# Half-row hand-overs between layers, a router's path folded into the last output unit, and one expert load issued earlier

## The chip, the cores and the metric

One NeuronCore of a Trainium2 chip runs the whole program, all in fp32. The metric is the device time of one execution in microseconds (us). The core's engines run from instruction queues of their own and wait for each other through semaphores: TensorE (PE, matrix products; PEld its weight loads), VectorE (DVE), ScalarE (ACT), GpSimd (POOL) and SyncE (SP), which here only issues DMA transfers. Products are written to PSUM, everything else lies in SBUF (128 partitions).

## The reference

A sequence of 256 tokens with 1024 channels passes through two blocks of two layers each. Cut to what matters:

```python
# first block, layer 0 (attention + SSM) and layer 1 (pooling); normed residual
for layer in range(2):
    y = mixer[layer](rmsnorm(x, pre_norm[layer]))        # products with w_in, w_out
    x = x + rmsnorm(y, post_norm[layer])
# second block
for layer in range(2):
    h = h + hybrid_mixer(rms_norm(h, norm1_g[layer]), ...)   # retention + HGRN2, w_in, w_out
    h = h + expert_choice_ffn(rms_norm(h, norm2_g[layer]), w_router, w_gate, w_up, w_down)
return rms_norm(h, final_norm_g)

def expert_choice_ffn(xn, w_router, w_gate, w_up, w_down):
    cap = 2 * s // 16                                    # 32 tokens for each of 16 experts
    affinity = softmax(xn @ w_router)
    gate, idx = top_k(swapaxes(affinity, 1, 2), cap)     # each expert chooses its tokens
    xe = gather(xn, idx)
    hid = silu(xe @ w_gate) * (xe @ w_up)
    ye = (hid @ w_down) * gate
    return scatter_add(ye, idx)
```

The weights of the 16 experts of one layer are 16 times 12 MB; each is used for 32 tokens only.

## The kernel before

The tokens lie as NT = 2 tiles of 128 rows (`x[:, i, :]`, i = 0, 1). Weights pass through a ring of 6 slots of 2 MB (`ring`), in "units": a unit is 2 MB (or 1 MB) of one weight matrix. Units 0 to 10 are even_w_in and the SSM's matrix, 11 to 13 even_w_out, 14 to 21 odd_w_in, 22 to 25 pool_w, 26 to 29 odd_w_out; FIRST2[l] (30 for layer 0 of the second block) starts nine units of w_in_2, OUT2[l] two of w_out_2, MOE[l] the 96 units of the experts (six for each: four of gate and up, two of down).

**Split units.** For nearly all dense units, weights and activations are split into a high part (rounded to fp32r) and a low part (the rest), and each product is three: L1475, L1476 and L1477. ScalarE makes the high part of a unit (`high_part`, L779, a 128x4096 copy), VectorE the low part (`low_part`, L1147). A split unit takes two ring slots. The first unit of layer 1 of the second block alone (`WHOLE`) is multiplied whole, in fp32 (L1492). A unit of output weights goes through `rows_unit`, in four quarters: token tile 0, columns 0 to 511 and 512 to 1023, then tile 1 the same.

**The seam between layers** of the first block (`norm_between`, on ScalarE L687, on VectorE L1001) comes after units 13 and 29. ScalarE squares and sums a row of the output in PSUM (`rms`, L681), VectorE scales it (L1005), adds it to x (L1008), ScalarE squares the sum, VectorE normalises into xs (L981), TensorE transposes xs (L1544) and VectorE makes the gained rows and their two parts (L993 product, L994 rounding, L995 subtraction) in `gain_out`. All of it whole rows of 1024, tile 0 and then tile 1.

**The router's path**, in each layer of the second block, comes after the second output unit. VectorE adds the output to x (L1369), TensorE transposes x (L1544, `transpose_rows`), VectorE applies the gain (L997), TensorE makes the logits (L1900), one tile after the other. Softmax (L1375 to L1379), transposes of the affinities (L1905), then the selection on VectorE (eight at a time, MAX8 and MATCH_REPLACE8, L1383 to L1388), transposes of the slot numbers (L1916), a copy (L1390), a comparison (`choose`, L1418) and the first gather on TensorE (L1927). TensorE also clears four PSUM banks by products with zeros (L1911), which stands between L1905 and L1916 in its queue.

**The experts.** Their units use the ring's 6 slots and three more (EXTRA) in the `work` area, which holds activations of the mixer until then. `load_moe` on SyncE issues the loads in the order of use; the three extra slots wait for `gm_sb` (both merges of the mixer's heads done), the first ring slots for the end of the units that used them, and every load from the tenth on for the end of the unit nine before. An expert is L1955 (gate and up, 32 instructions for each unit in the trace), L1927 for the next gather, L1980 (down) and L1992 (scatter).

**What sets the order.** Each engine's order is written out by hand. TensorE's smaller steps are hung into the dense units at fixed quarters (`ahead_of`, `slots`).

## Time and profile before

| | us |
|---|---|
| median of 3 runs | 1712.32 |
| lowest and highest of them | 1712.03, 1713.57 |
| profiled execution, own time | 1711.37 |
| its span | 1709.6 |
| TensorE busy | 1333.4 (78%) |
| VectorE busy | 559.1 (33%) |
| ScalarE busy | 424.6 (25%) |
| bytes moved by DMA | 516.38 MB, mean 302 GB/s |

The span lies 1.8 us below the execution's own time. Times in the rows are microseconds from the span's start. A row of the timeline gives start, duration, engine, line, operation and shapes; in brackets stands how long the engine was idle before it and what ended that. Chains are read by laying the end of one engine's row beside the start of the next engine's. TensorE's instructions are pipelined, so that rows overlap by some tenths.

The page's chain that ended last goes to 47% through DMA transfers (nearly all of them expert weights) and to 39% through TensorE.

### The profile page before, as it was taken

Reading aid. Unit: us, or ns where it says so; the run is one execution under the profiler, and the core shown is the slowest. Engines: PE = TensorE matmul, PEld = TensorE weight load, DVE = VectorE, ACT = ScalarE, POOL = GpSimd, SP = SyncE. Lnnn points to the kernel's source line nnn. Section 1 sums busy time; section 2 is a strip of 40 time slices with the busy share of each in tenths; the row PEclk is TensorE's granted clock in tenths of the full one; section 3 lists DMA queues with packets and bytes.
Section 4 is the critical chain, followed back from the end, with each engine's and each line's share of the span. In section 5 each row is a group of like instructions: output and inputs, shape, how many; then the busy total and the mean of one; then the engine's idle time right before and its main releaser. Section 6 shows DMA issues by size and latency. Waiting matters only on the chain.

```text
span 1709.6 us, 28214 instructions
## 1 busy us (share of the span) xinstructions
PE 1333.4 (78%) x12496; PEld 923.3 (54%) x12496; DVE 559.1 (33%) x790; ACT 424.6 (25%) x538; POOL 136.4 (8%) x155
## 2 busy tenths in 40 slices
PE   7999889999899987665665666999986666566564
PEld 5688767998798853232322233788843223223232
DVE  8855775455566430000000001485520000000001
ACT  5236334443465311000101011455210101000011
POOL 0120300000304000000000000204000000000000
PEclk9999999999999989798889887999989888888886
DMA  9134243564443699999999999333799999999996
GB/s 326 51 124 148 111 164 114 174 219 149 147 149 124 245 398 426 424 428 425 427 425 427 426 426 411 133 137 133 286 408 425 426 427 424 428 424 428 425 426 264
DMA packets 86148, 516.38 MB, mean 302 GB/s; under 512 B 6336, under 2 KB 6464, under 8 KB 53056
## 3 DMA queue, kind: packets, MB, share of 16 engines
q1 hardware_dynamic: 82576, 509.20, 73.3%
q0 software_dynamic: 992, 3.42, 0.6%
q10 hardware_dynamic: 2512, 2.75, 0.5%
q8 instruction: 55, 0.90, 0.2%
q14 instruction: 13, 0.11, 0.0%
HBM read 514.30 MB, written 1.05 MB: 301 GB/s over the span
## 4 chain that ended last, share of the span: by engine, by line
DMA 47%; PE 39%; DVE 6%; POOL 2%; ACT 2%; issue 2%; SPq 1%; DVEq 0%; ACTq 0%; POOLq 0%
DMA ring<-in_w_down 24%; DMA ring<-in_w_gate 20%; PE dense L1475 8%; PE dense L1477 8%; PE dense L1476 8%; PE bank L1955 3%; DMA ring<-in_w_up 2%; PE dense L1492 2%; PE bank L1980 2%; DMA ring<-in_even_w_in 1%; PE bank L1814 1%; DVE ring_parts L1147 1%; POOL work L655 1%; PE bank L1900 1%; PE dense L1911 1%
## 5 line engine op out<-in xcount | busy, mean ns | idle before, releaser
L1955 PE MATMUL bank<-ring,work 128*32 128x256 f32 x2688 | 203.3, 457 | 143.9 <-DMA ring<-in_w_up 87.7
L1955 PEld LDWEIGHTS bank<-ring,work 128*32 128x32 f32 x2688 | 92.3, 126 | 249.6 <-DMA ring<-in_w_up 108.5
L1147 DVE TENSOR_TENSOR ring_parts<-ring,ring_parts 128x4096 fp32r<-128x4096 f32 (+1 forms) x44 | 184.1, 4194 | 115.8 <-ACT ring_parts L779 115.7
L951 ACT ACTIVATE work<-bank 128x256 f32<-128x256 f32 x32 | 12.3, 384 | 750.5 <-PE bank L1955 750.5
L1407 DVE TENSOR_TENSOR work<-work,bank 128x256 f32<-128x256 f32 x32 | 13.5, 421 | 563.0 <-ACT work L951 563.0
L779 ACT ACTIVATE ring_parts<-ring 128x4096 fp32r<-128x4096 f32 (+1 forms) x45 | 154.1, 3432 | 96.2 <-DMA ring<-in_w_in 40.4
L1955 PE MATMUL bank<-work 128*32 128x256 f32 x1408 | 105.8, 454 | 71.2 <-DMA work<-in_w_up 45.1
L1980 PE MATMUL bank<-ring,work 128*32 128x256 f32 x1344 | 91.8, 419 | 59.6 <-DMA ring<-in_w_down 54.9
L1475 PE MATMUL dense<-xT_parts,ring_parts 128*128 128x256 f32 x448 | 129.5, 289 | 2.7 <-DVE ring_parts L1147 2.7
L1477 PE MATMUL dense<-xT_parts,ring_parts 128*128 128x256 f32 x448 | 126.8, 283 | 0.0
L1955 PEld LDWEIGHTS bank<-work 128*32 128x32 f32 x1408 | 49.9, 127 | 124.8 <-DMA work<-in_w_up 55.7
L1476 PE MATMUL dense<-work_parts,ring_parts 128*128 128x256 f32 x400 | 113.2, 283 | 0.0
L1477 PE MATMUL dense<-ring_parts,work_parts 128*128 128x512 f32 x288 | 112.9, 392 | 0.0
L664 POOL TENSOR_TENSOR work<-work 128x128 f32<-128x128 f32 x64 | 24.2, 399 | 933.9 <-PE bank L1963 782.2
L1980 PEld LDWEIGHTS bank<-ring,work 128*32 128x32 f32 x1344 | 43.0, 119 | 100.5 <-DMA ring<-in_w_down 67.2
L1412 DVE COPY work<-bank 128x256 f32<-128x256 f32 x32 | 13.6, 424 | 228.6 <-PE bank L1980 228.6
L1475 PEld LDWEIGHTS dense<-xT_parts,ring_parts 128*128 128x128 f32 x448 | 85.9, 192 | 3.6 <-ACT work L699 3.1
L1477 PEld LDWEIGHTS dense<-xT_parts,ring_parts 128*128 128x128 f32 x448 | 85.9, 192 | 0.0
L1475 PE MATMUL dense<-ring_parts,xT_parts 128*128 128x512 f32 x176 | 72.9, 414 | 8.9 <-DVE xs_parts L995 3.9
L1476 PEld LDWEIGHTS dense<-work_parts,ring_parts 128*128 128x128 f32 x400 | 76.7, 192 | 0.4 <-issue 0.2
L1475 PE MATMUL dense<-ring_parts,work_parts 128*128 128x512 f32 x176 | 69.9, 397 | 2.3 <-ACT work L704 2.3
L1476 PE MATMUL dense<-ring_parts,xT_parts 128*128 128x512 f32 x176 | 69.7, 396 | 0.0
(325 smaller groups left out, 2202.5 us busy)
## 6 DMA issues: line engine op xcount, KB each, us to landing
ring<-in_w_gate SPq DMA_DIRECT2D x42, 2048.0 KB, 41.0
ring<-in_w_up SPq DMA_DIRECT2D x42, 2048.0 KB, 41.0
ring<-in_w_down SPq DMA_DIRECT2D x42, 2048.0 KB, 40.8
work<-in_w_gate SPq DMA_DIRECT2D x22, 2048.0 KB, 40.6
work<-in_w_up SPq DMA_DIRECT2D x22, 2048.0 KB, 40.7
work<-in_w_down SPq DMA_DIRECT2D x22, 2048.0 KB, 41.1
ring<-in_w_in SPq DMA_DIRECT2D x18, 2048.0 KB, 8.6
ring<-in_even_w_in SPq DMA_DIRECT2D x10, 2048.0 KB, 10.6
```

The lines of the kernel that those rows point to most:

```text
L655: g.tensor_tensor(x1, t4[0], t4[1], ALU.subtract).then_inc(rot_done, 1)
L664: g.tensor_tensor(wsel[:, i], csel[:, i:i + 1, :].to_broadcast([P, 4, CAP]), aff[:, i, bass.ds(e, 1)].unsqueeze(2).to_broadcast([P, 4, CAP ...
L779: s.activation(slot_of(u, True)[0], slot_of(u), ACT.Copy).then_inc(hi_done, 1)
L1147: tt(lo, slot_of(u), hi.bitcast(F32), ALU.subtract).then_inc(lo_done, 1)
L1475: mm(o, x_parts[0], y_parts[0], start=start, stop=False)
L1476: mm(o, x_parts[0], y_parts[1], start=False, stop=False)
L1477: return mm(o, x_parts[1], y_parts[0], start=False, stop=stop)
L1492: last = mm(d[:, i, :], act_T[:, k, i, :], w[:, k, :], start=k == 0, stop=k == nk - 1)
L1814: last = mm(o, x_, y_, start=True, stop=True)
L1900: last = mm(WB[0][:, NE * i:NE * i + NE], xT[:, k, i * P:(i + 1) * P], wr[:, l, k, :], start=k == 0, stop=k == DC - 1)
L1955: last = mm(WB[0][32 * q:32 * q + 32, 256 * (j % 2):256 * (j % 2) + 256], xeT[:, 4 * (j // 2) + k, :], w[:, k * D + 256 * q:k * D + 256 * ...
L1980: last = mm(WB[3][32 * r:32 * r + 32, 0:256], hidT[:, b, 32 * q:32 * q + 32], w[:, at:at + 256], start=q == 0 and b == 0, stop=q == 3 and ...
```

## The change

Five pieces.

1. **Half rows in `norm_between`.** Squares, scaling and addition run by halves of 512 columns, `half_ps` and `sum_half` announce the first ones; a half's sum enters the second half's root as its bias. In `gain_out` VectorE only makes the product and the subtraction; the rounding copy goes to ScalarE (`gain_high`). `normalise` writes two halves, and `transpose_rows` waits for each.
2. **The seam between the two layers of the second block**: the first unit (`WHOLE`) starts when tile 0's rows are gained (`full_ready`); tile 1's transposes stand inside it, the roundings and subtractions behind all four products.
3. **The router's path**: `rows_unit` of the last output unit takes eight transposes of tile 0 ahead of its fourth quarter, and ahead of that quarter's last k (`late`) tile 0's logits and half of tile 1's transposes. The clearing of the PSUM banks takes fp32r operands and stands before the affinities' transposes. The first choice is compared straight from PSUM. Tile 1's scaling stands between softmax and selection.
4. **Expert loads**: the load j = 4 (FIRST_IN) is issued ahead of the output units and waits for `ho_ps`; the loads into the other two extra slots wait for the end of the mixer's last input unit and for the first merge. `rgT` and `hgT` are moved out of those slots.
5. **The output** leaves in two transfers, one for each tile.

```diff
-        rgT = area(13312, "p (h s) -> p h s", h=RH, s=S)
-        hgT = area(14336, "p (h s) -> p h s", h=RH, s=S)
+        rgT = area(4096, "p (h s) -> p h s", h=RH, s=S)
+        hgT = area(11264, "p (h s) -> p h s", h=RH, s=S)
...
-                        sp.wait_ge(gm_sb, 4 * (l + 1))
+                        sp.wait_ge(*((unit_done, OUT2[l]), (gm_sb, 4 * l + 2), (ho_ps, l + 1))[s - RING])
...
+                FIRST_IN = RING - 2
+                load_moe(0, FIRST_IN)
+                for u in range(OUT2[l], MOE[l]):
+                    load(u)
                 for j in range(6 * TURN_E):
-                    load_moe(j // 6, j)
+                    if j != FIRST_IN:
+                        load_moe(j // 6, j)
...
+                dense_rms(0)
+                sum_rms(0)
+                dense_rms(1)
+                gain_high(0, at)
+                sum_rms(1)
+                gain_high(1, at)
+
+            def rms_halves(i, of, first, second):
+
+                act.wait_ge(*first)
+                own.link(s.activation(xs[:, i, 0:512], of[:, 0, :], ACT.Square, accum_out=stat[:, 7, 0:1]))
+                own.go(s.activation(stat[:, 7, 1:2], stat[:, 7, 0:1], ACT.Identity, scale=1.0 / D, bias=eps[:]))
+                act.wait_ge(*second)
+                own.link(s.activation(xs[:, i, 512:1024], of[:, 1, :], ACT.Square, accum_out=ssq[:, i:i + 1]))
+                s.activation(std[:, i:i + 1], ssq[:, i:i + 1], ACT.Sqrt, scale=1.0 / D, bias=stat[:, 7, 1:2]).then_inc(std_ready, 1)
...
-                for i in range(NT):
-                    if i == 0:
-                        dve.wait_ge(tile0_ps, 3 + l)
-                    else:
-                        dve.wait_ge(unit_done, MOE[l])
-                    tt(x[:, i, :], x[:, i, :], DP[i][:].rearrange("p b n -> p (b n)"), ALU.add).then_inc(x_ready, 1)
-                    gain_out(i, f"n2_{l}")
-                for i in range(NT):
-                    normalise(i)
-                v.memset(zeros, 0.0).then_inc(zero_set, 1)
+                tt(zeros, ident, ident, ALU.subtract).then_inc(zero_set, 1)
+                dve.wait_ge(tile0_ps, 3 + l)
+                add_half(0, 0)
+                add_half(0, 1)
+                dve.wait_ge(half_ps, 6 + 2 * l)
+                add_half(1, 0)
+                gain_out(0, f"n2_{l}")
+                normalise(0)
+                dve.wait_ge(unit_done, MOE[l])
+                add_half(1, 1)
+                gain_out(1, f"n2_{l}")
+                inverse(1)
...
+                ts(xs[:, 1, :], x[:, 1, :], rstd[:, 1:2], None, ALU.mult).then_inc(xs_ready, 2)
...
-                              [[], [], [at(mix_transposes, 0)], []] if n == 0 else ())
+                              [[], [], [at(mix_transposes, 0)], []] if n == 0 else [[], [], [], [first_rows]],
+                              [[], [], [], [first_logits]] if n else ())
+                rows_half(1, 1)
+                logits(1, 0)
+                logits(1, 1).then_inc(lg_ps, 1)
```

**TensorE, router's path.** Before, from the end of the last output unit to the transposes of the slot numbers (bank, dense: PSUM; x: the tokens; wr: router weights; con, work: constants and activations):

```order
L1544 MATMUL bank<-con,x 128x128 x8
L1900 MATMUL bank<-wr,xT 128x16 x8
L1544 MATMUL bank<-con,x 128x128 x8
L1900 MATMUL bank<-wr,xT 128x16 x8
L1905 MATMUL bank<-con,work 16x128 x2
L1911 MATMUL dense<-xT,work 128x512 x4
L1916 MATMUL bank<-con,work 128x16 x2
```

Of the change, the same stretch, from the first logits, which now stand inside that unit:

```order
L1959 MATMUL bank<-wr,xT 128x16 x8
L1948 MATMUL bank<-con,x 128x128 x4
L1541 MATMUL dense<-ring_parts,work_parts 128x512
L1542 MATMUL dense<-ring_parts,work_parts 128x512
L1543 MATMUL dense<-ring_parts,work_parts 128x512
L1948 MATMUL bank<-con,x 128x128 x4
L1959 MATMUL bank<-wr,xT 128x16 x8
L2003 MATMUL dense<-work_parts 128x512 x4
L2008 MATMUL bank<-con,work 16x128 x2
L2013 MATMUL bank<-con,work 128x16 x2
```

Tile 0's logits and four of tile 1's transposes stand ahead of the unit's last three products (eight more transposes stand a quarter earlier), and the clearing (L1911, now L2003) has changed places with the affinities' transposes.

**VectorE, first seam, tile 0.** Before, from the first reciprocal to the last low part:

```order
L976 RECIPROCAL rstd<-std 128x1
L1005 SCALAR_TENSOR_TENSOR xs<-dense,rstd,row 128x1024
L1008 TENSOR_TENSOR x<-x,xs 128x1024
L976 RECIPROCAL rstd<-std 128x1
L981 TENSOR_SCALAR xs<-x,rstd 128x1024
L993 TENSOR_TENSOR xs<-bank,vec 128x512
L994 CAST xT_parts<-xs 128x4x128
L995 TENSOR_TENSOR xs_parts<-xs,xT_parts 128x512
L993 TENSOR_TENSOR xs<-bank,vec 128x512
L994 CAST xT_parts<-xs 128x4x128
L995 TENSOR_TENSOR xs_parts<-xs,xT_parts 128x512
```

Of the change:

```order
L1008 RECIPROCAL rstd<-std 128x1
L1044 SCALAR_TENSOR_TENSOR xs<-dense,rstd,row 128x512
L1050 TENSOR_TENSOR x<-x,xs 128x512
L1044 SCALAR_TENSOR_TENSOR xs<-dense,rstd,row 128x512
L1050 TENSOR_TENSOR x<-x,xs 128x512
L1008 RECIPROCAL rstd<-std 128x1
L1015 TENSOR_SCALAR xs<-x,rstd 128x512 x2
L1025 TENSOR_TENSOR xs<-bank,vec 128x512 x2
L1034 TENSOR_TENSOR xs_parts<-xs,xT_parts 128x512 x2
```

The two rounding copies (CAST) have left VectorE's queue, and the scaling and the addition stand in two halves each.

**SyncE, loads around the output units of layer 0.** Before:

```order
L549 DMA ring<-in_w_out_2 128x4x1024 x2
L580 DMA ring<-in_w_gate_2 128x4096
L580 DMA ring<-in_w_up_2 128x4096
L580 DMA work<-in_w_gate_2 128x4096
L580 DMA work<-in_w_up_2 128x4096
L580 DMA work<-in_w_down_2 128x2x2048
```

Of the change:

```order
L587 DMA work<-in_w_down_2 128x2x2048
L555 DMA ring<-in_w_out_2 128x4x1024 x2
L587 DMA ring<-in_w_gate_2 128x4096
L587 DMA ring<-in_w_up_2 128x4096
L587 DMA work<-in_w_gate_2 128x4096
L587 DMA work<-in_w_up_2 128x4096
```

One load of down weights has moved ahead of the two loads of output weights.

## Rows read from the trace of the kernel before

**Rows 1.** Page, part 2: busy share of the 16 DMA engines in 40 slices, in tenths.

```profile
DMA  9134243564443699999999999333799999999996
```

**Rows 2.** Timeline, VectorE, first seam (before unit 14): start, us, line, out<-in, [idle before].

```profile
245.86 1.28 DVE L1005 SCALAR_TENSOR_TENSOR xs<-dense,rstd,row 128x1024 f32<-128x1024 f32 x1
247.18 1.23 DVE L1008 TENSOR_TENSOR x<-x,xs 128x1024 f32<-128x1024 f32 x1
...
250.21 0.75 DVE L981 TENSOR_SCALAR xs<-x,rstd 128x1024 f32<-128x1024 f32 x1
251.71 0.69 DVE L993 TENSOR_TENSOR xs<-bank,vec 128x512 f32<-128x512 f32 x1 [0.75 <-PE bank L1544]
...
252.90 0.69 DVE L995 TENSOR_TENSOR xs_parts<-xs,xT_parts 128x512 fp32r<-128x512 f32 x1
...
254.69 0.69 DVE L995 TENSOR_TENSOR xs_parts<-xs,xT_parts 128x512 fp32r<-128x512 f32 x1
...
264.32 0.69 DVE L995 TENSOR_TENSOR xs_parts<-xs,xT_parts 128x512 fp32r<-128x512 f32 x1
```

**Rows 3.** Timeline, ScalarE: full-row square in that seam, half-row square elsewhere.

```profile
248.44 1.06 ACT L681 ACTIVATE xs<-x 128x1024 f32<-128x1024 f32 x1 [2.88 <-DVE x L1008]
...
539.75 0.60 ACT L919 ACTIVATE rtmp<-bank 128x512 f32<-128x512 f32 x1
```

**Rows 4.** Second seam: ScalarE's timeline; then waits of TensorE, 445 to 590 us.

```profile
442.50 3.61 ACT L779 ACTIVATE ring_parts<-ring 128x4096 fp32r<-128x4096 f32 x1
...
PE dense L1475 <- DVE ring_parts L1147: 2.7, 1, 2.7
```

**Rows 5.** Windows of that first seam: busy (count) by engine, then PEclk, DMA share, GB/s.

```profile
255.00:258.00 3.00, 2.56 (x6) 2.08 (x7) 2.93 (x4) 0.00 (x0) 0.00 (x0) 0.50 0.55 214
```

**Rows 6.** Timeline, TensorE, first layer's path from the last output unit to the experts.

```profile
599.62 1.03 PE L1544 MATMUL bank<-con,x 128*128 128x128 f32 x8
...
601.60 2.27 PE L1900 MATMUL bank<-wr,xT 128*128 128x16 f32 x16 [0.94 <-DVE xT L997]
...
606.44 3.60 PE L1900 MATMUL bank<-wr,xT 128*128 128x16 f32 x16 [0.78 <-DVE xT L997]
...
612.23 5.84 PE L1911 MATMUL dense<-xT,work 128*128 128x512 f32 x8
...
618.93 2.02 PE L1927 MATMUL bank<-xs,work 128*32 128x256 f32 x16 [0.64 <-DVE work L1418]
...
622.54 3.66 PE L1955 MATMUL bank<-ring,work 128*32 128x256 f32 x64 [0.60 <-DVE work L1401]
```

**Rows 7.** Timeline, VectorE, the same path.

```profile
612.48 0.42 DVE L1383 MAX8 work<-bank 16x8 f32<-16x256 f32 x1 [0.69 <-PE bank L1905]
...
617.35 0.41 DVE L1388 TENSOR_TENSOR work<-work 16x256 f32<-16x256 f32 x1
```

**Rows 8.** Timeline, SyncE's queue: first load that waits for an expert's slot.

```profile
624.53 0.33 SPq L580 DMA_DIRECT2D ring<-in_w_up  x1
```

**Rows 9.** Windows on that path: busy (count) by engine, then PEclk, DMA share, GB/s.

```profile
616.00:618.00 2.00, 2.00 (x4) 0.50 (x2) 1.66 (x4) 0.00 (x0) 0.00 (x0) 0.82 1.04 442
622.00:624.00 2.00, 1.46 (x28) 0.98 (x32) 0.53 (x2) 0.00 (x0) 0.00 (x0) 1.00 0.52 221
```

**Rows 10.** Timeline, TensorE, expert stage: two units of 32 products.

```profile
746.45 3.59 PE L1955 MATMUL bank<-ring,work 128*32 128x256 f32 x32 [2.96 <-DMA ring<-in_w_gate]
751.34 1.93 PE L1955 MATMUL bank<-ring,work 128*32 128x256 f32 x32 [1.30 <-DMA ring<-in_w_up]
```

**Rows 11.** Between the layers: TensorE's timeline, then VectorE's.

```profile
1071.19 14.00 PE L1492 MATMUL dense<-ring,xs 128*128 128x512 f32 x32 [1.20 <-DVE work_parts L995]
...
1074.63 4.42 DVE L1147 TENSOR_TENSOR ring_parts<-ring,ring_parts 128x4096 fp32r<-128x4096 f32 x1
```

**Rows 12.** DMA issues by line: out<-in, count, KB each, median us to landing.

```profile
x<-in_x SPq DMA_DIRECT2D x2, 512.0 KB, 4.1
...
out<-xs SPq DMA_DIRECT2D x1, 1024.0 KB, 4.1
```

168 lines of the change are left out of this document (113 added, 55 removed).

## The prediction

> **What bounds the kernel now.** Read first the page's row of DMA shares [rows 1]: digits of 9 from slice 15 to 24 and from 30 to the end are the two expert stages, in which the 16 DMA engines never rest. All before and between them is bound by TensorE and by the hand-overs between engines, the "seams". Second, the timeline of each seam: what stands between the last product of one unit and the first of the next. Third, SyncE's queue: when the expert loads are released.
>
> In an expert stage nine slots of 2 MB are filled ahead, and each further load waits until TensorE has finished with a slot. The first that waits is issued at 624.53 [rows 8]; in the window around it the DMA share drops to 0.52 [rows 9]. So nine slots were full and the stream stood still: the stage's end follows the moment of TensorE's first finished expert unit, not the moment of the first load.
>
> **The seams before units 14 and 30 (norm, add, norm).** The chain per token tile is: ScalarE squares, VectorE scales and adds, ScalarE squares the sum, VectorE normalises, TensorE transposes, VectorE makes gained rows in two parts.
> - Squares: 1.06 for a row, 0.60 for a half [rows 3]. The first half now runs while the second is still being made: -0.46, twice.
> - VectorE: 1.28 + 1.23 + 0.04 between them [rows 2] = 2.55. Four halves at 0.69, 0.65, 0.69, 0.65 (0.69 is the half-row price of L993 in the same rows; 0.65 is half of 1.23 and 0.04 of start) and three gaps of 0.04 make 2.80: +0.25.
> - Normalising: 0.75 for a row [rows 2]; the transposes of the first half may begin after some 0.41: -0.34.
> - Gained rows: from 251.71 to 254.69 + 0.69 = 3.67 [rows 2], for six instructions. Now two products and two subtractions, four times 0.72 = 2.88, with the rounding copies on ScalarE at 0.60 beside them: -0.8.
>
> Tile 0: -0.46 + 0.25 - 0.46 - 0.34 - 0.8 = -1.8. For tile 1 the first square was already done ahead: -1.35. Tile 0's copies stand in ScalarE's queue behind tile 1's first statistics, which costs some 0.15. Sum -3.0. Does it reach TensorE? In the first seam TensorE takes tile 1's rows when the last VectorE instruction ends (264.32 + 0.69 [rows 2]). In the second, TensorE later waited 2.7 for the low part of unit 31 (L1147) whose high part starts at 442.50, right behind the last VectorE instruction of the seam [rows 4]. So both pass on the whole: **-6.0** for two seams. Bounds: -4.0, if the halves cost 0.25 more per instruction pair than I take, and -7.5: the clock stood at 0.50 in 255 to 258 after the long pause [rows 5], which is TensorE's 1.2 of 2.4 GHz, and a shorter pause may leave it at 1.00 (it then gains little, since VectorE's tile 1 ends last).
>
> **The router's path, once per layer.** Before: the last output product ends near 599.85, its start pipelined into the transposes of 599.62, the logits end at 606.44 + 3.60 = 610.04, the selection runs from 612.48 to 617.35 + 0.41 = 617.76, the first gather starts at 618.93 and the first expert unit ends near 624.5 [rows 6 to 8].
> - TensorE now puts eight transposes (1.03), tile 0's logits (2.27) and four more transposes (0.5) [rows 6] inside the last output unit, which so ends at 599.85 + 3.8 = 603.65. What follows is short: half a row added (0.65), four transposes (0.5 at full clock, 0.95 at half), half a row gained (0.69), the last eight logits rows (half of 2.27 or of 3.60 [rows 6]). Logits end at 607.1 at full clock, 608.7 at half: -2.95 or -1.35.
> - One scaling (0.75 [rows 2]) now stands before the selection, beside two transposes that took about as long: +0.1.
> - Selection to gather took 618.93 - 617.76 = 1.17. The zeroing ended at 618.07 (612.23 + 5.84 [rows 6]), later than the selection, and no longer stands there (0.3); the first choice is now read straight from PSUM, without the copy ahead (0.1): -0.4.
>
> So the gather starts 1.65 (half clock) or 3.25 (full clock) sooner. I weigh them 2 to 1, since the second logits took 3.60 where the first took 2.27, the work between them being as thin as it will be: -2.2. **But the zeroing was also what brought the clock back.** It began at 0.50 and ended at 1.00: the window 616 to 618 has 0.82 [rows 9]. Now it is short and stands before the selection; TensorE then has nothing for over 5 us. Nearest row for a start after idleness: 32 products take 3.59 after 2.96 us of waiting, 1.93 at full clock [rows 10]. A gather of 2.02 [rows 6] at that ratio is 3.76: +1.75; two transposes at the same ratio some +0.25; the first expert unit +0 to +1.7, taken as +0.15, since the gather's own work comes first. Penalty +2.15. Net **-0.1 for both layers**; bounds +2.05 and -3.25 each.
>
> The Trainium skill ("TensorE: Matmul & The Clock Gate", Part 1, what is actually happening) says that the slow clock is the default and that activity releases it, idleness brings it back. The rule speaks against moving the zeroing; rows 9 and 10 agree with it. By the opposite assumption, a clock that stays, the path would give -3.25 a layer.
>
> **The extra slot.** One expert load goes ahead of the output weights, two more no longer wait for the second merge. That fills the ring some 6 us earlier, but the ring was already full when the first unit ended [rows 8, 9], so it earns nothing by itself: 0. It only raises the cap on what a faster router could earn (0.96 us of idle DMA in the window 622 to 624, and about as much until the load of 624.53 gets going). Its 2 MB stand ahead of the first output weights (4.8 us at the 442 GB/s of rows 9), which ScalarE splits at 550 and VectorE not before 565: hidden.
>
> **Between the layers.** TensorE's first unit (14.00 [rows 11]) now starts after tile 0's two products on VectorE alone. The two roundings and two subtractions between them fall away (3.6 to 1.45, as in the first seam) and the transposes begin 0.34 sooner: start -2.5. Tile 1's eight transposes move inside it (+1.0), and it starts with less work ahead of it, so partly at half clock: for a time between nothing and the 4.5 us of the zeroing, taken as 2.4, which costs +1.2. VectorE's low part for the next unit (4.42 [rows 11]) comes after four roundings that now stand later, and ends about when the unit does. Net **-0.3**; bounds -1.7 and +1.3.
>
> **The end.** Output in two halves: 1 MB landed in 4.1, but so did 0.5 MB at the start [rows 12]. Half of the bytes at 442 GB/s are 1.2 less; bounds 0 and -1.4. I take **-1.0**.
>
> **Sum.** The profiled execution took 1711.37 (span 1709.6). -6.0 - 0.1 - 0.3 - 1.0 = -7.4: 1704.0. The median of the runs shown, 1712.32, lies 0.95 above it, so I predict **1704.9** (ratio 0.9957). About 0.2% (3.4 us) is what a measurement of this kernel can tell from no change.
>
> **Rivals.**
> 1. *The router's path wins in full* (the clock holds, or comes back within the gather). For it: TensorE is busier through the logits than before. Against: over 5 us of idleness before the gather. -3.25 instead of -0.05, twice: 1704.9 - 6.4 = 1698.5. Chance 0.15.
> 2. *Half clock up to the first expert unit* in both layers: +2.05 instead of -0.05, twice: 1704.9 + 4.2 = 1709.1. For it: row 746.45 stays slow to its end [rows 10]. Against: the clock came back after some 4.5 us of work, between 612.23 and 616.7 (0.82 in the window from 616 [rows 9]). Chance 0.22.
> 3. *The halves earn half*: instruction overhead eats the seams, 1704.9 + 3 = 1707.9. Against: half-row prices are in the rows. Chance 0.08.
> 4. *Slower than before*: the unit between the layers starts on a cold array and stays at half clock. At its price of 14.00 for the whole unit at full clock, each us at half clock costs 0.5; the whole unit would add 14.0 - 1.2 = 12.8: 1717.7. It decides from some 17 us at half clock (7.4 saved elsewhere is used up at 14.8 beyond my 2.4); the return at 612 took 4.5. Chance 0.03.
> 5. *The forecast*, 1702 to 1708: chance 0.52.
>
> The range takes in 1 and most of 2: **1698.5 to 1709.5**. Faster by over 0.2% (below 1708.9): 0.52 + 0.15 + 0.08 + about half of case 2, less a little: 0.82. Within 0.2%: 0.14. Slower: 0.04.
>
> **What would show it.** Seams: the last subtraction of the first seam ends 3 us sooner after the start of its first scaling, and the start of unit 31 has moved with the second one. Router: logits end 10 to 11.6 us after the third quarter of the last output unit's products instead of 13; the gather takes 3 to 4 us, not 2.0; SyncE's first waiting load comes about as long after the output unit's third quarter as before (some 27.4 us). If the gather still takes 2.0, rival 1 is right. Extra slot: a longer gap of the DMA before the first expert unit ends, not a shorter stage. I am wrong if a waiting engine that I left out ends last: ScalarE between tile 1's statistics and tile 0's copies, or VectorE's low part behind unit 31 or between the layers.

## The result, and the profile after

| | before | after |
|---|---|---|
| median, us | 1713.57 (5 runs, 1712.03 to 1716.78) | 1703.57 (5 runs, 1700.19 to 1706.39) |
| profiled execution; its span | 1711.37; 1709.6 | 1706.39; 1704.5 |
| VectorE, ScalarE busy | 559.1, 424.6 | 558.3, 433.9 |

The ratio is 0.9945, 95% interval 0.9922 to 0.9967: the changed kernel is 9.4 us faster, with an interval from 5.7 to 13.4. I had forecast 1704.9 and a ratio of 0.9957. The total is right, but its terms are not. Two seams that I had put at -3.0 each gave -1.2 and -2.6. The router's path, which I had put at -0.1 for both layers, is the largest term: -4.8 in these two profiles.

The DMA row of the page of the changed kernel, which answers [rows 1], has an 8 in slices 15 and 30, the first of each expert stage, where a 9 stood before (before, the first stage's nines are slices 15 to 25, not to 24 as I wrote):

```profile
DMA  9134334455354589999999999444689999999996
```

**First seam**, timeline of the changed kernel, VectorE on tile 1 (it answers [rows 2]). Columns: start and duration in us, engine, line, operation, out<-in, count, and in brackets the idle time before and what ended it.

```profile
264.46 1.29 DVE L1025 TENSOR_TENSOR xs<-bank,vec 128x512 f32<-128x512 f32 x2 [0.37 <-PE bank L1615]
265.85 1.29 DVE L1034 TENSOR_TENSOR xs_parts<-xs,xT_parts 128x512 fp32r<-128x512 f32 x2
269.97 8.76 DVE L1190 TENSOR_TENSOR ring_parts<-ring,ring_parts 128x4096 fp32r<-128x4096 f32 x2 [2.82 <-ACT ring_parts L811]
```

ScalarE at the same place:

```profile
265.19 1.23 ACT L725 ACTIVATE xT_parts<-xs 128x512 fp32r<-128x512 f32 x2 [2.31 <-DVE xs L1025]
266.32 7.13 ACT L811 ACTIVATE ring_parts<-ring 128x4096 fp32r<-128x4096 f32 x2
```

TensorE, the first product of unit 15:

```profile
274.54 0.47 PE L1541 MATMUL dense<-ring_parts,xT_parts 128*128 128x512 f32 x1 [1.50 <-DVE ring_parts L1190]
```

Two products and two subtractions take 1.29 + 1.29 here, and VectorE's chain is as much shorter as I had worked out: from the start of ScalarE's square of tile 0's last half (before: of its row) to the end of tile 1's last subtraction it took 20.90 before and takes 17.84 now. But VectorE then stands still for 2.82, because the high part of unit 15 (the first of the two of 266.32) is made only behind the copies of 265.19, and TensorE waits 1.50 at the start of unit 15. In the kernel before this wait does not exist.

**Second seam.** Before, ScalarE stood still ahead of two sigmoids (L858, L859) that wait for a subtraction on VectorE (L1254) behind the whole seam, and only then made the high part of [rows 4]:

```profile
442.29 0.21 ACT L858 ACTIVATE lbt<-lbt 128x4 f32<-128x4 f32 x1 [4.27 <-DVE lbt L1254]
```

ScalarE's timeline in the changed kernel (it answers the first line of [rows 4]):

```profile
441.08 1.24 ACT L725 ACTIVATE xT_parts<-xs 128x512 fp32r<-128x512 f32 x2 [2.29 <-DVE xs L1025]
442.33 1.28 ACT L890 ACT_TABLE_LOAD   x1
443.62 0.21 ACT L890 ACTIVATE lbt<-lbt 128x4 f32<-128x4 f32 x1
443.74 0.19 ACT L891 ACTIVATE lbt<-lbt 128x4 f32<-128x4 f32 x1
443.83 7.12 ACT L811 ACTIVATE ring_parts<-ring 128x4096 fp32r<-128x4096 f32 x2
```

VectorE's low parts for units 31 and 32 behind it:

```profile
447.48 8.76 DVE L1190 TENSOR_TENSOR ring_parts<-ring,ring_parts 128x4096 fp32r<-128x4096 f32 x2 [4.36 <-ACT ring_parts L811]
```

The one wait of TensorE between 440 and 470 (total us, times, longest), as in [rows 4]:

```profile
PE dense L1541 <- DVE ring_parts L1190: 3.1, 1, 3.1
```

And a window behind it: busy time of PE, PEld, DVE, ACT and POOL with counts, granted clock, DMA share, GB/s.

```profile
452.00:455.00 3.00, 2.95 (x14) 2.98 (x15) 3.00 (x1) 0.00 (x0) 3.00 (x1) 0.50 1.05 406
```

The wait ahead of unit 31 has grown from 2.7 to 3.1: a table load of 1.28 and two sigmoids stand between the copies and the high part of unit 31. Before, the same table load ran while ScalarE waited in any case. Behind the wait the clock was at 0.50.

**Router's path**, first layer, TensorE's timeline (it answers [rows 6]):

```profile
606.90 2.09 PE L1959 MATMUL bank<-wr,xT 128*128 128x16 f32 x16
608.83 2.05 PE L2003 MATMUL dense<-work_parts 128*128 128x512 f32 x4
616.83 0.39 PE L2013 MATMUL bank<-con,work 16*128 16x16 f32 x2 [5.38 <-DVE work L1439]
617.63 2.05 PE L2024 MATMUL bank<-xs,work 128*32 128x256 f32 x16 [0.41 <-DVE work L1442]
620.29 0.69 PE L2033 MATMUL bank<-con,work 128*128 128x128 f32 x2 [0.61 <-DVE work L1450]
621.57 5.64 PE L2052 MATMUL bank<-ring,work 128*32 128x256 f32 x64 [0.60 <-DVE work L1455]
```

SyncE's first load that waits for an expert's slot ([rows 8]):

```profile
625.27 0.33 SPq L587 DMA_DIRECT2D ring<-in_w_up  x1
```

Three windows up to it ([rows 9]):

```profile
619.30:621.30 2.00, 1.07 (x6) 0.29 (x2) 0.71 (x2) 0.00 (x0) 0.00 (x0) 0.50 0.08 33
621.30:623.30 2.00, 1.73 (x19) 0.82 (x23) 0.27 (x2) 0.00 (x0) 0.00 (x0) 0.50 0.00 0
623.30:625.30 2.00, 2.00 (x24) 0.97 (x20) 0.00 (x0) 0.00 (x0) 0.00 (x0) 0.50 0.00 0
```

The second logits took 2.09 instead of 3.60. The gather of 617.63 ran at a granted clock of 0.50 and took 2.05, not the 3.76 of my forecast. The first expert unit did run slow, 5.64 instead of 3.66. The DMA rests for 6 us ahead of the load of 625.27 (its share was 0.48 in 618 to 620 and 0.00 from 622).

**Between the layers**, TensorE's unit with tile 1's transposes inside ([rows 11]):

```profile
1067.59 6.27 PE L1558 MATMUL dense<-ring,xs 128*128 128x512 f32 x8 [0.78 <-DVE xs L1505]
1073.69 1.04 PE L1615 MATMUL bank<-con,xs 128*128 128x128 f32 x8
1074.57 10.46 PE L1558 MATMUL dense<-ring,xs 128*128 128x512 f32 x24
```

A window in its first quarter:

```profile
1067.00:1070.00 3.00, 2.41 (x3) 1.18 (x4) 1.49 (x4) 1.85 (x1) 0.00 (x0) 0.50 1.04 384
```

**The end**, timeline of SyncE's two output transfers and of VectorE's last instruction:

```profile
1700.07 1.75 SPq L603 DMA_DIRECT2D out<-xs  x2
1700.15 1.28 DVE L1519 SCALAR_TENSOR_TENSOR xs<-x,rstd,row 128x1024 f32<-128x1024 f32 x1
```

The unit between the layers took 6.27 + 10.46 = 16.7 of products where it took 14.00 before; its first quarter ran at half clock.

### The stretches

Every engine's order is fixed, so a stretch between two marks can be compared over all traces. The marks: S1 and S2, the start of ScalarE's square that tile 0's last half (before: its row) releases at the first and second seam; Q0 and Q1, the start of ScalarE's square of tile 0 in each router's path (L681, after: L694). All in us, each the difference of two starts in one trace (the end of a unit is the start of the copy that it releases; the last row ends with the span, which is known to a tenth); "again" is a second profile of the kernel before (run e5).

| stretch | before | again | after | e1 | e2 | e3 | e4 |
|---|---|---|---|---|---|---|---|
| start to S1 | 244.12 | 245.22 | 249.30 | 248.68 | 247.38 | 246.42 | 248.22 |
| S1 to the first copy of a pool product (in unit 15) | 30.77 | 30.78 | 29.57 | 30.23 | 29.56 | 29.57 | 29.42 |
| S2 to unit 31's first product | 29.43 | 29.43 | 26.83 | 28.90 | 26.84 | 26.83 | 23.60 |
| S2 to the head norms' root (stat 128x8), 155 us on | 156.76 | 156.78 | 155.46 | 157.70 | 155.65 | 154.13 | 150.84 |
| Q0 to the first waiting load | 28.84 | 28.85 | 26.87 | 24.78 | 24.91 | 24.74 | 24.74 |
| Q1 to the same in layer 1 | 27.79 | 27.62 | 24.94 | 25.02 | 24.94 | 24.90 | 24.99 |
| that load to TensorE's last landed weights, layer 0 | 431.93 | 432.37 | 432.10 | 432.33 | 433.04 | 432.08 | 432.05 |
| the same, layer 1 | 433.37 | 434.34 | 433.36 | 433.28 | 434.33 | 433.36 | 433.36 |
| ScalarE's statistics to the end of the unit between the layers | 21.50 | 23.30 | 22.55 | 22.95 | 23.05 | 23.02 | 22.64 |
| last statistics (first square) to the end | 9.01 | 8.94 | 7.55 | 7.56 | 7.57 | 7.59 | 7.55 |

Between these rows lie stretches that the change does not touch. From the first seam's mark in unit 15 to S2, from the head norms to Q0 and from the unit between the layers to Q1 they repeat within 0.25; from the last landed weights to ScalarE's statistics they read 5.2 to 7.3 in the first layer and 5.2 to 7.8 in the second. The code there is the same in all kernels, and what differs is the granted clock under the last expert units: before, it was at 0.50 from 1057.0 on, after, at 1.00 until 1062.5.

Because of the clock the two profiles must not be compared as a whole. From S1 on they differ by 10.3. Of this 2.8 lie in those last stretches (7.3 and 5.2, 7.8 and 7.1). In the other direction the changed kernel had half clock for 4.0 us of its first expert unit (2.1 longer), as no other trace has, and in unit 31 (1.3 longer than in e3). The latter befell three of the six traces that wait ahead of unit 31 (after, e1, e2) and none of the six that do not (e4 and all on top of it).

### The profile page after: what moved, and what is told of

It is laid out like the page before. It is cut to its first block, busy times and chain, and to the rows that moved or that the text cites. A ratio compares the mean times of both kernels' runs of the same rounds, so it can differ in the third digit from the quotient of the medians.

```text
span 1704.5 us, 28251 instructions
## 1 busy us (share of the span) xinstructions
PE 1323.7 (78%) x12488; PEld 920.2 (54%) x12488; DVE 558.3 (33%) x804; ACT 433.9 (25%) x570; POOL 139.1 (8%) x155
## 4 chain that ended last, share of the span: by engine, by line
DMA 47%; PE 40%; DVE 5%; POOL 2%; ACT 2%; issue 2%; SPq 1%; DVEq 0%; ACTq 0%; POOLq 0%
DMA ring<-in_w_down 25%; DMA ring<-in_w_gate 22%; PE dense L1541 8%; PE dense L1543 8%; PE dense L1542 8%; PE dense L1558 2%; PE bank L2052 2%; PE bank L2077 2%; DVE ring_parts L1190 1%; PE dense L1575 1%; ACT ring_parts L811 1%; DMA ring<-in_even_w_in 1%; PE bank L1888 1%; POOL work L668 1%; PE bank L1760 1%
## 5 line engine op out<-in xcount | busy, mean ns | idle before, releaser
L2052 PE MATMUL bank<-ring,work 128*32 128x256 f32 x2688 | 204.6, 459 | 157.3 <-DMA ring<-in_w_up 95.8
L2052 PE MATMUL bank<-work 128*32 128x256 f32 x1408 | 105.6, 454 | 66.4 <-DMA work<-in_w_up 42.2
L2077 PE MATMUL bank<-ring,work 128*32 128x256 f32 x1344 | 84.0, 391 | 52.7 <-DMA ring<-in_w_down 43.9
L1541 PE MATMUL dense<-ring_parts,xT_parts 128*128 128x512 f32 x176 | 72.5, 412 | 7.3 <-DVE work_parts L1034 2.3
L2077 PE MATMUL bank<-work 128*32 128x256 f32 x704 | 50.1, 433 | 27.2 <-DMA work<-in_w_down 24.2
```

The source lines that it names most:

```text
L1541: mm(o, x_parts[0], y_parts[0], start=start, stop=False)
L2052: last = mm(WB[0][32 * q:32 * q + 32, 256 * (j % 2):256 * (j % 2) + 256], xeT[:, 4 * (j // 2) + k, :], w[:, k * D + 256 * q:k * D + 256 * ...
L2077: last = mm(WB[3][32 * r:32 * r + 32, 0:256], hidT[:, b, 32 * q:32 * q + 32], w[:, at:at + 256], start=q == 0 and b == 0, stop=q == 3 and ...
```

## The experiments

Each was timed several times beside the kernel before on the same chip, and the ratio is to that one; e5 and e10 were run once. Where one stands on top of another, that is said.

### e5: the kernel before, once more (one run)

> The kernel before itself, once more, for a second sample of its own trace. From the start to ScalarE's square of tile 0 ahead of the first seam, where the change moves nothing, the first profile of before took 244.12 us and five profiles of the changed kernel and its variants 246.42 to 249.30; the first unit's 64 products took 14.08 there and 16.55 here. Theory: that is chance of TensorE's clock, so this second profile lies between 244 and 250 too, likely near 247, while each stretch behind the first seam repeats the first profile within 0.3 us, except where a dip of the clock falls (first seam 30.8, second seam to the end of its first unit 28.2, third quarter of the output unit to the first waiting load 28.8 and 27.8, last landing to the end of the unit between the layers 28.8 give or take 2). Rival: the change does move something at the start, and this profile has 244.1 again with a first unit of 14.08; then the changed kernel loses some 3 us there that an edit could win back.

1713.91 us. From the start to S1 it took 245.22. Its first unit, in TensorE's timeline:

```profile
15.07 15.24 PE L1509 MATMUL dense<-xT,ring 128*128 128x256 f32 x64
```

The same 64 products in the changed kernel:

```profile
16.43 16.56 PE L1575 MATMUL dense<-xT,ring 128*128 128x256 f32 x64 [2.39 <-DMA ring<-in_even_w_in]
```

In eleven traces other than the first of before this unit took 15.24 to 16.98, and S1 stood at 243.81 to 249.30, in both kernels. So the first profile of before (14.08 and 244.12) was at the lucky end, and the 5.2 us by which the profile of after is behind at S1 lie inside the spread that one and the same code shows up to there. (The changed kernel normalises its first rows in halves; an effect of a microsecond from that is not excluded by two traces of before.) Part of it is the landing of the first weights: the unit started at 14.73 before and at 16.43 after, behind a wait of 2.39. Part is where TensorE's granted clock falls to 0.50 for a moment: after, e1 and e4 have such a dip near 188 and another near 225, e3 has none before 256. The Trainium skill ("TensorE: Matmul & The Clock Gate", Part 1, what's actually happening) says that how many of a kernel's first products run at the slow clock varies from run to run; the spread of this one unit, 14.08 to 16.98, agrees. In the window from 19 to 21 the unit of before (14.08) ran at a granted clock of 1.00, that of after (16.56) at 0.50. From S1 to the end the kernel before took 1465.5 and 1466.9, the changed one 1455.2. The timed medians differ by 10.0 (by the ratio 9.4), close to this difference and not to the 5.0 of the two profiled executions.

### e1: the two seams as before

```diff
-                dense_rms(0)
-                sum_rms(0)
-                dense_rms(1)
-                gain_high(0, at)
-                sum_rms(1)
-                gain_high(1, at)
+                for i in range(NT):
...
+                    rms(i, DP[i][:].rearrange("p a b -> p (a b)"))
+                    act.wait_ge(x_ready, 2 * (k - 1) + i + 1)
+                    rms(i, x[:, i, :])
```

(and in VectorE's `norm_between` and `gain_out` the same way back). Not everything goes back: the normalised rows are still written in two halves, and TensorE's transposes still wait for each half.

> One part of the change undone: the seams ahead of unit 14 and unit 30 work in whole rows again, VectorE making the high parts itself; the router, the loads, the seam between the layers and the end stay as in the changed kernel. Theory, from the two traces laid side by side (tile 0 done to the end of the two units behind the seam): the halves earned 1.2 us at the first seam and between 1.4 and 2.75 at the second, so this kernel is 2.6 to 4.0 us above the changed kernel's 1703.6: 1706.2 to 1707.6. Rival one, the terms of my sum: 3.0 at each seam, 1709.6. Rival two, the shorter VectorE chain is swallowed whole by the new waits on ScalarE: the same time as the changed kernel within 0.2%, 1703.6. In the trace the stretch from ScalarE's first square of the first seam to the end of the second unit behind it should be about 28.1 us again, and about 29.4 behind the second.

1706.64 us, ratio 0.9965 (0.9953 to 0.9977); the changed kernel has 0.9945 (0.9922 to 0.9967). By the medians of the ratios the halves earn 3.4 us, near the theory (2.6 to 4.0) and under my forecast's 6.0, though the intervals overlap. The table says it more sharply: 30.23 against 29.57 at the first seam, 28.90 against 26.83 at the second, 2.7 together. (The stretches of 28.1 and 29.4 in the expectation were counted to other marks; those of the table are the ones to go by.) The halves were worth 1.2 and 2.6 against the kernel before, 0.7 and 2.1 against this one; the 0.5 between the two at each seam is the normalised half row that e1 keeps (VectorE's chain of 20.90 is 20.37 in e1 and 17.83 with all halves).

### e4: ScalarE's queue in another order

```diff
                 sum_rms(1)
+                high_half(last + 2, 0)
                 gain_high(1, at)
...
             norm_between(13, 1)
-            high_part(15)
+            high_half(15, 1)
...
-            act.wait_ge(lb_diff, 1)
-            s.activation(lbt[:, 1, :], lbt[:, 0, :], ACT.Sigmoid).then_inc(lb_sig, 1)
-            s.activation(lbt[:, 2, :], lbt[:, 0, :], ACT.Sigmoid, scale=-1.0).then_inc(lb_sig, 1)
...
-                high_part(u + 1)
+                if l:
+                    high_part(u + 1)
+                else:
+                    high_half(u + 1, 1)
```

(`high_half(u, h)` makes one half of the columns of unit u's high part; the two sigmoids go ahead of the first decay of the mixer, where a sigmoid table is loaded anyway. So the first seam has one edit, the second two, which no run separates.)

> ScalarE's order at the two seams changed and nothing else: half of the high part of the unit behind the next (unit 15, unit 31) is made between tile 1's last statistics and its copies, where ScalarE waits for VectorE, and the other half behind the copies; the two sigmoids of the load balance, with the table load ahead of them (1.28 us), move off the second seam. Theory: the halves earned less than the 3.0 us forecast for each seam because that high part now stands behind the copies in ScalarE's queue; TensorE's waits for the low part made from it (1.50 and 3.1 us) shrink to nothing and to about 1.5, and the kernel gains about 1.5 us at each seam, 3 in all: 1700.6. If the clock also stays at full speed in unit 31, 1.3 more: 1699.3. Rival one: VectorE's low part isn't waiting for ScalarE but for its own gain work, and nothing moves: 1703.6. Rival two: the half that stands ahead of the copies delays them by its 1.8 us where ScalarE has less than that to spare, and tile 1's transposes and gains end later: slower by up to 1 us at each seam, 1705.6.

1696.20 us, ratio 0.9910 (0.9893 to 0.9928): 6.0 us below the changed kernel by the ratios, twice what the theory had, and the two intervals overlap only at the edge. The traces say what of it is the edit. ScalarE's timeline at the second seam of this kernel:

```profile
437.47 1.90 ACT L821 ACTIVATE ring_parts<-ring 128x2048 fp32r<-128x2048 f32 x1
439.86 1.23 ACT L726 ACTIVATE xT_parts<-xs 128x512 fp32r<-128x512 f32 x2 [0.49 <-DVE xs L1041]
441.00 1.90 ACT L821 ACTIVATE ring_parts<-ring 128x2048 fp32r<-128x2048 f32 x1
442.80 3.61 ACT L812 ACTIVATE ring_parts<-ring 128x4096 fp32r<-128x4096 f32 x1
```

VectorE's low parts behind it:

```profile
442.93 8.76 DVE L1206 TENSOR_TENSOR ring_parts<-ring,ring_parts 128x4096 fp32r<-128x4096 f32 x2 [1.03 <-ACT ring_parts L821]
```

The first half of the high part fits in where ScalarE had waited 2.29 for VectorE's product; the copies wait 0.49 for it and are not late; VectorE's low part begins 1.03 after its last subtraction, where it was 4.36. TensorE has no wait left ahead of unit 31 or of unit 15. From S2 to unit 31 it is now 23.60 (26.83 in the changed kernel, 29.43 before), and the mark 155 us on shows 150.84: 4.6 less than after, of which 1.3 is the clock in unit 31 (e3, which waits as long, has 154.13), and 5.9 less than before. At the first seam this trace has 29.42, because here the clock stood at 0.50 while TensorE transposed tile 1 (1.86 for the eight transposes of 262.66, 1.09 for eight at full clock). The five other kernels with this edit have 27.81 to 27.86: 2.95 less than before, which is my forecast's 3.0 for a seam. So the halves do shorten VectorE's chain by what I had worked out, and the changed kernel loses 1.7 of it at the first seam to the high part in ScalarE's queue. By the traces the edit is worth 1.7 and 3.2, 4.9 in all, where I had expected 1.5 at each seam: the wait of 3.1 went whole. Unit 31's 1.3 comes on top wherever the wait would have brought half clock. Part of that wait is older than the change (2.7 before), and whether the moved sigmoids or the halves of the copy removed it is open.

### e2: the extra slot taken back

```diff
-                        sp.wait_ge(*((unit_done, OUT2[l]), (gm_sb, 4 * l + 2), (ho_ps, l + 1))[s - RING])
+                        sp.wait_ge(gm_sb, 4 * (l + 1))
...
-                FIRST_IN = RING - 2
-                load_moe(0, FIRST_IN)
```

> One part of the change undone: the extra slot. The expert weights are loaded in their earlier order and wait for the gathered weights of all four quarters, as in the kernel before; all else is the changed kernel. Theory: the slot covers nothing in this kernel, because TensorE's first expert unit doesn't wait for its weights and the stage's end is set by the DMA stream, which resumes with the same wait: the time is the changed kernel's 1703.6 within 0.2%, and the DMA gap ahead of the first expert unit is shorter than the changed kernel's 618 to 626.5 by about the 4.1 us of one slot's transfer, with the expert stage longer by the same. Rival: the slot is what lets the shorter router path count; then the 1.7 and 2.6 us that the two router paths became shorter are lost in part, and the time is 1705 to 1708.

1703.66 us, ratio 0.9953 (0.9936 to 0.9970): 1.4 above the changed kernel, which the timed runs cannot tell from nothing. The trace can. The three windows that end at the first waiting load (621.53 in this trace):

```profile
615.50:617.50 2.00, 1.79 (x16) 0.64 (x16) 0.16 (x2) 0.00 (x0) 0.76 (x2) 0.50 0.98 418
617.50:619.50 2.00, 0.84 (x6) 0.29 (x2) 0.94 (x3) 0.00 (x0) 0.00 (x0) 0.70 1.02 434
619.50:621.50 2.00, 1.96 (x36) 1.25 (x40) 0.04 (x1) 0.00 (x0) 0.00 (x0) 1.00 0.94 401
```

Without the slot the DMA does not rest at all, while with it it rests for 4 to 6 us in the first layer. The load comes at the same moment (24.91 and 24.94), but the last weights land later: 433.04 and 434.33 instead of 432.1 and 433.4. So my theory (nothing) fell, and the rival was right in kind: some transfers are still under way when the load is issued, worth 0.9 in the first layer. In the second it reads 1.0, but there the second profile of before has 434.34 as well, so that figure is not safe.

### e9: the extra slot taken back from the fastest kernel

The same edit on top of e8 (below).

> The fastest kernel so far (ScalarE's new order, products of zeros behind the affinities and ahead of the unit between the layers; 1693.7 us), with the extra slot undone: expert loads in their earlier order and with their earlier waits. Theory, formed on the first kernel without the slot, where the stretch from the first waiting load to the last landing grew by 0.94 in the first layer and 0.97 in the second while the wait itself moved by less than 0.1: with the shorter router path the DMA is no longer idle when that load is issued, so one more transfer ahead of it is worth what the path gained beyond the old gap, 1.0 us a layer at full clock in the logits, and nothing in a layer where the logits of tile 1 run at half clock (the path is then 26.4 instead of 24.7). So 1694.7 to 1695.7, and stretches of 433.0 and 434.3. Rival, my forecast's term: the slot earns nothing, the ring is full either way: 1693.7 and stretches of 432.1 and 433.4.

1693.60 us, ratio 0.9895 (0.9876 to 0.9914), e8 beside its own runs of before 0.9880 (0.9866 to 0.9894): 2.6 us slower by the ratios, not resolved; the median itself is below the 1694.7 to 1695.7 that I had expected. The stretches are 432.93 and 434.53, where the eight traces with the slot and the shorter path have 432.04 to 432.39 and 433.26 to 433.63. All four stretches without the slot lie above all sixteen with it, so the rival (nothing) is out by the traces; what the slot saves in time is worked out from them, the timed runs do not resolve it.

### e3: products of zeros during the selection

```diff
                 last.then_inc(aff_ps, 1)
+                for _ in range(3):
+                    for r in range(4):
+                        mm(yb[r], zeros, m_hi[:, 0:2, :].rearrange("p c s -> p (c s)"), start=True, stop=True)
```

> An addition: twelve more products of zeros into the cleared banks behind the transposes of the affinities, while VectorE selects, so that TensorE isn't idle there. In the changed kernel the granted clock falls to 0.50 ahead of the gather in both layers; the gather still took 2.05 us, but in the first layer the first expert units ran at half clock (5.64 us against 3.66). Theory: with the products the gather again takes about 2.05 (its time is not set by the clock), the first layer's first expert unit takes 3.7 and the kernel gains 1.8 us at most in that layer, none in the second where the units were at full clock already: 1701.8 to 1703.6. Rival one: the stage's length is set by its DMA stream, so that a faster first unit only waits for its weights: same as the changed kernel, 1703.6, with the wait grown by 1.8 us. Rival two: the products hold up the gather's start because they are still running when the selection is done: slower by their time beyond the selection, up to 1 us in each layer, 1704.5 to 1705.6.

1700.77 us, ratio 0.9936 (0.9920 to 0.9951), not to be told from 0.9945. Its first layer:

```profile
613.26 2.02 PE L2027 MATMUL bank<-xs,work 128*32 128x256 f32 x16 [0.41 <-DVE work L1442]
616.94 3.66 PE L2055 MATMUL bank<-ring,work 128*32 128x256 f32 x64 [0.60 <-DVE work L1455]
```

The window over the gather:

```profile
613.00:616.00 3.00, 2.12 (x17) 0.59 (x18) 0.64 (x3) 0.00 (x0) 0.76 (x2) 1.00 0.58 246
```

At a granted clock of 1.00 the gather takes 2.02; in the changed kernel, at 0.50, it took 2.05. So its time hardly depends on the clock. The profile of before had already held this, in a gather of a later expert:

```profile
812.94 2.07 PE L1927 MATMUL bank<-xs,work 128*32 128x256 f32 x16
812.90:814.70 1.80, 1.80 (x20) 0.60 (x12) 0.42 (x1) 0.39 (x1) 0.00 (x0) 0.50 0.98 410
```

The added products do not hold the clock reliably. In the four kernels that have them (e3, e7, e8, e9) the gather of the first expert ran at 1.00 in four layers of eight and at about 0.50 in the others, the second layer of e3 among them (2.03). The path to the load is 24.74 and 24.90, and so is it in e1, e2 and e4, which have no such products and a gather at half clock; there the clock came back ahead of the first expert unit. It did not in the first layer of the profile of the changed kernel, whose path is 2.1 longer for it (26.87).

### e7: the same products on top of e4

> On top of the same kernel (1696.2 us), the twelve products of zeros behind the transposes of the affinities. Theory: they save nothing where the clock is full at the first expert unit anyway (three of four profiled executions without them), and 2.1 us where it isn't, because the first load that waits for a slot is issued when the first half of that unit is done; so the median gains 0 to 1 us (1695.2 to 1696.2), the highest of the times comes down, and the path from the third quarter of the last output unit to that load is 24.7 and 24.9 us in both layers. Rival: the gather is held up by the products; then the path is 25 to 26 and the time 1697 to 1698.

1695.50 us, ratio 0.9886 (0.9871 to 0.9901) against 0.9910 of e4: nothing told apart; the highest of four times is 1697.5, against 1700.1 for six of e4. The expectation missed the first layer: 26.45, not 24.7. There the second logits took 3.43 at a clock of 0.50, as in e6 and e8, and this is ahead of the added products. What these can mend is small: with such logits and no products (e6) the path was 26.87.

### e10: the clearing of the banks back behind the affinities (one run, on top of e4)

```diff
-                pe.wait_ge(zero_set, l + 2)
...
                 last.then_inc(aff_ps, 1)
+                pe.wait_ge(zero_set, l + 2)
```

(with the four products behind it).

> On top of the kernel with ScalarE's new order (1696.2 us, path from the third quarter of the last output unit to the first waiting load 24.7 and 25.0 us): the clearing of the banks goes back behind the transposes of the affinities, where the kernel before had it, in its new short form of four products. Theory: the affinities' transposes and with them the selection start sooner by nothing, since the clearing lay ahead of them in a wait that VectorE's affinities end (at full clock) or almost (at half clock, 0.8 later); the gather is then at 19.0 after the third quarter, at full or half clock alike 2.05 long; the clock before the first expert unit may be up or down. So 24.5 to 25 in both layers at full clock in the logits, 26.0 where those are at half clock. Rival, from my forecast: the clearing is what brings the clock back, so that moving it back makes the gather faster than 2.02 or the first expert unit reliably 3.66 where otherwise it is 5.6.

1693.35 us; 24.86 and 24.94. TensorE in the first layer:

```profile
599.63 2.05 PE L2023 MATMUL dense<-work_parts 128*128 128x512 f32 x4
605.35 0.39 PE L2029 MATMUL bank<-con,work 16*128 16x16 f32 x2 [3.67 <-DVE work L1455]
606.15 2.05 PE L2040 MATMUL bank<-xs,work 128*32 128x256 f32 x16 [0.41 <-DVE work L1458]
609.93 3.66 PE L2068 MATMUL bank<-ring,work 128*32 128x256 f32 x64 [0.60 <-DVE work L1471]
```

The place of the clearing changes nothing: gather 2.05, first expert unit 3.66. This does not test the long clearing of before (5.84). That one may well have brought the clock up: in both traces of before it was back at 1.00 ahead of the gather, in the changed kernel's only behind it. What I feared from its loss, a slow gather, does not occur, and a slow first expert unit occurred once.

### e6: the seam between the layers as before, on top of e4

```diff
-                (full_rows if l else tile_in_xT)()
+                if l == 1:
+                    transpose_x(1)
+                tile_in_xT()
```

(and VectorE makes both tiles' parts ahead of the unit).

> On top of the kernel with ScalarE's new order at the two seams (1696.2 us), the seam between the two layers undone: VectorE makes high and low parts of both tiles ahead of the unit, both tiles' transposes come first, as in the kernel before. Theory: the new seam starts the unit 2.4 us sooner but runs its first half at half clock (16.7 us for the unit against 14.0) with 1.0 of transposes inside, so that from ScalarE's statistics to the end of the unit it takes 22.6 where the old one took 21.5: undone, the kernel is 1.1 us faster, 1695.1, below what the rounds can tell apart, but the stretch in the trace reads 21.5. Rival, my forecast's term: the new seam earns 0.3, so undone it is 1696.5 and the stretch is 22.9. Second rival: the old seam too runs at half clock when the pause ahead of it is as long as here; then the stretch is 24 to 25 and the kernel 1698 to 1699.

1695.42 us, ratio 0.9895 (0.9876 to 0.9913), e4 0.9910: the same within the intervals. The stretch is 23.50, above the 21.5 that I expected; the second profile of before has 23.30. So the old seam takes 21.50 to 23.50 and the new one 22.44 to 23.05: this part of the change earned nothing that can be seen, by the clock's doing. (The old seam ran its unit in 14.00 at full clock in one trace and in 15.8 and 15.9 in two; the new one started on half clock in all seven traces without added products ahead of it.)

### e8: a warmed unit between the layers, and the fastest kernel

On top of e7:

```diff
+                for _ in range(8 if l else 0):
+                    mm(WB[2][:], zeros, m_hi[:, 0:2, :].rearrange("p c s -> p (c s)"), start=True, stop=True)
                 transpose_x(0)
                 (full_rows if l else tile_in_xT)()
```

> On top of the same kernel (1696.2 us), both the twelve products of zeros behind the affinities' transposes and eight products of zeros ahead of the first transposes of the unit between the layers, meant to raise TensorE's clock there. Theory: the unit between the layers took 16.7 us with its first 5 at a granted clock of 0.50, and 14.0 at full clock plus 1.0 of transposes is 15.0; if the eight products bring the clock up, the stretch from the statistics to the unit's end falls from 22.6 to 21 and the kernel to 1694 or 1695. Rival one: eight products are too few or come too late, because TensorE waits again behind them for VectorE's gained rows, and the clock falls anew: stretch 22.6, time as with the products behind the affinities alone. Rival two: they stand in front of tile 0's transposes and delay them by up to 1.6 us: stretch 24, time 1697 to 1698.

1693.72 us, ratio 0.9880 (0.9866 to 0.9894): 20.6 us below the kernel before and about 11 below the changed one. TensorE's timeline around the unit:

```profile
1050.98 2.11 PE L1878 MATMUL bank<-work_parts 128*128 128x512 f32 x8
1054.81 1.09 PE L1631 MATMUL bank<-con,xs 128*128 128x128 f32 x8 [1.72 <-DVE xs L1031]
1056.84 3.70 PE L1574 MATMUL dense<-ring,xs 128*128 128x512 f32 x8 [0.94 <-DVE xs L1521]
1060.38 1.04 PE L1631 MATMUL bank<-con,xs 128*128 128x128 f32 x8
1061.26 10.47 PE L1574 MATMUL dense<-ring,xs 128*128 128x512 f32 x24
```

The window in its first quarter:

```profile
1057.00:1060.00 3.00, 3.00 (x8) 1.33 (x9) 0.78 (x2) 3.00 (x1) 0.00 (x0) 1.00 1.06 390
```

The eight products take 2.11 out of a wait that was 3.75 in the changed kernel, and the clock is at 1.00 throughout. The first quarter takes 3.70 instead of 6.27, and the stretch is 19.27 (19.26 in e9), where I had expected 21: 3.2 less than in e7, which lacks only these products, 3.4 less than in e4 and 2.2 less than the old seam at its best. At full clock the new seam is worth about what I had put on its start (2.5).

## Why the prediction came out right, and where it was wrong

Predicted 1704.9, measured 1703.57; by ratio 0.9957 and 0.9945. The sign and the range hold; that the total is so near is luck, as the terms show:

- **First seam, -3.0: gave -1.2.** The working of VectorE's chain holds (20.90 to 17.84 up to the last subtraction, and -2.95 at the mark in unit 15 once ScalarE's order is mended, e4). The step that failed is "both pass on the whole". I had followed VectorE to its last subtraction and not asked what ScalarE does next. Before, the high part of unit 15 ran at 259.45, under VectorE's work; after, the copies that I had moved to ScalarE stand ahead of it. My last sentence named ScalarE and VectorE's low part as what could end last, but without a price.
- **Second seam, -3.0: gave -2.6** up to unit 31. The same step, and a table load of 1.28 that had run under cover. I had read the high part of [rows 4] as following VectorE's last instruction of the seam; it followed two sigmoids, which wait for that instruction. e4 moved them too and took away the whole wait. The unit behind the wait then ran at either clock (in the changed kernel 1.3 longer than in e3).
- **Router's path, -0.1 for both layers: gave -2.0 to -4.1 in the first and -2.8 in the second.** Two steps were wrong, in the same direction. (a) The gather's start: I had -1.65 at half clock in the logits and -3.25 at full, weighed to -2.2. Measured from Q0, the gather began at 23.24 before, at 18.98 to 19.23 in seven traces with fast logits (-4.0 to -4.3) and at 20.76 to 20.88 in three with slow ones (-2.4); from Q1, at 22.02 to 22.20 before and 18.88 to 19.10 in all ten (-3.1). I had let the output unit end 3.8 later for the work hung into it, with tile 0's logits at 2.27; they took 1.85 and the start of each piece ran into the end of the last, so that the logits of tile 1 ended 0.9 sooner than I had. And I had taken slow logits as twice as likely, where they were the exception: 3 of 20 paths of the changed kernel and its variants (all four of the kernel before, at 3.60). (b) The penalty of +2.15 for a cold array: the gather's +1.75 came from the ratio of rows 10. It took 2.05 at half clock and 2.02 at full. The rows could have told: at full clock the gather's 16 products take 0.126 each, more than the 0.112 that an expert unit's product of the same printed shape takes at half clock (3.59 for 32), so something other than the array's clock sets their pace. The two differ in more than the clock: the gather reads every eighth column of xs, the expert unit 256 numbers in a row; no run separates this. The transposes cost up to 0.25 more, as I had it; the first expert unit cost 2.1 in one trace of the changed kernel's first layer and nothing in most. Rival 1 (the path wins in full, 0.15) has the right size and the wrong reason: it wanted the clock to hold or to come back within the gather, and I had written that a gather of 2.0 would show it. The gather took 2.05 with the clock at 0.50 from its start to its end.
- **Extra slot, 0: the path's gain would have been cut by 0.9 a layer without it** (first layer; the second is open). I had said that it raises the cap on what a faster router can earn, and that the gap of the DMA grows, which it does in the first layer, from about 1.4 to 4 to 6 us. With my own router's term of -0.05 a layer there was nothing to cap; this 0 fell with that term.
- **Between the layers, -0.3: nothing visible** (22.44 to 23.05 against 21.50 and 23.30). The start was 2.4 sooner and the transposes 1.0, as forecast; half clock cost 2.7 for 1.2.
- **The end, -1.0: gave -1.4**, my lower bound.

Added up from S1 on, the change is worth 1465.5 - 1455.2 = 10.3 on the first profile of before, and 7.5 without the last expert units, whose 2.8 are the clock's. That this is my sum of 7.4 is luck: too much by 2.2 at the seams, too little by 4.7 on the router, and half clock in unit 31 and in the unit between the layers took back another 2.6. I had also read 1711.37 as a typical execution. Its start was one of the luckiest of twelve, and chance of 2 to 5 us is hidden in any comparison of two single profiles.

## What to carry to other kernels

When work moves from the engine that ends last to another, follow the receiving engine's queue past it: the next thing it did under cover is now late, and here its place in the queue (at one seam with that of two sigmoids) was worth more than the change it mended: by the traces 4.9 us, against 2.7 for what e1 undoes of the halves. Before pricing a group of products at the slow clock, compare its time for one with that of a group of the same shape known to be slow: if it is longer already, something else sets its pace. And look for the same group elsewhere in the profile at half clock; here it stood in the profile of before. Where an engine must wait anyway, a few products of zeros ahead of a large fp32 unit can win more than anything else in the seam (2.1 us hidden in the wait, 3.2 won, in both traces that have them); behind a small step they won nothing that could be measured. Compare stretches between fixed marks over several traces before giving a difference of two profiles to the change.

## What the runs showed of the hardware

- The first gather's 16 products took 2.02 to 2.03 at a granted clock of 1.00 and 2.03 to 2.05 at 0.50 or close to it, while the first expert unit's 64 of the same printed shape took 3.66 and 5.64 (at 0.50 for most of it), and the logits 1.96 and 3.44. What sets the gather's pace stays open; its strided read of xs is untested.
- With the same code up to S1 but for the first normalisation (whole rows before, half rows after), that stretch took 243.81 to 249.30 in twelve traces; the later stretches repeat within 0.25 us except where the clock dips. How much of the first stretch's spread is the clock and how much the landing of the first weights (its first unit started at 14.73 to 17.04) is not separated.
- In the changed kernel and its variants without the added products, where TensorE idles for some 3.7 or 5.4 us during the selection, the clock was 0.50 in the gather in all twelve layers. It was back at 1.00 ahead of the first expert unit or within 0.2 us of its start in eleven of them, and in one it stayed at 0.50 for 4.0 us of that unit.
